# Forgetting attention moved whole out of RWKV's loop into the later projections, with its two products turned round

## The reference

```python
z = h @ w_in[i]
q = rmsnorm_2(q, g_qnorm[i]); k = rmsnorm_2(k, g_knorm[i])
for start in range(0, s_len, Q_BLOCK):            # Q_BLOCK = 128
    end = start + Q_BLOCK
    sc = einsum('bqhd,bkhd->bhqk', q[:, start:end], k[:, :end]) * scale
    sc = where(kpos <= qpos, sc + c[start:end] - c[:end], -1e30)   # c: running sum of log forget gates
    outs.append(einsum('bhqk,bkhd->bqhd', softmax(sc), v[:, :end]))
zr = zr + mu_shift[i] * (token_shift(zr) - zr)    # RWKV's columns, shifted by a token
... # RWKV: decay and a through two small products ("lora"), a recurrence over the tokens
merged = sigmoid(zg_fox) * (y_fox @ w_o_fox) + sigmoid(zg_rwkv) * (y_rwkv @ w_o_rwkv)
```

## Time and profile before

| | us |
|---|---|
| median of 3 runs | 4296.64 |
| the profiled execution | 4300.37 |
| its span | 4299.1 |
| TensorE busy | 3922.4 (91%) |
| VectorE busy | 2143.1 (50%) |
| ScalarE busy | 1157.1 (27%) |
| POOL busy | 330.0 (8%) |

### The profile page before, as it was taken

How to read it: one execution, slowest core, us unless ns; L and a number is a source line. 1 busy time by engine, 2 the same in 40 slices (tenths; PEclk the granted TensorE clock), 3 DMA queues, 4 the chain that set the end, 5 groups by cost and what they waited for, 6 DMA issues and landing times. The chain is left out here.

```text
span 4299.1 us, 75536 instructions
## 1 busy us (share of the span) xinstructions
PE 3922.4 (91%) x33542; PEld 3206.1 (75%) x33542; DVE 2143.1 (50%) x3525; ACT 1157.1 (27%) x1597; POOL 330.0 (8%) x362
## 2 busy tenths in 40 slices
PE   6999959986998999999999999778887999999999
PEld 5788837774876888888798677566666788888877
DVE  4633345554433444445624333465554476666774
ACT  4221234442322312121400222242323321111122
POOL 0001102230000000000000000232311000000000
PEclk8999969997998999999999899888787999999999
DMA  5212120114112111111132312201004311111111
GB/s 179 87 52 69 50 84 6 32 32 150 49 40 98 48 51 40 50 48 49 51 133 96 125 67 84 87 23 56 22 10 149 108 48 41 49 49 49 50 45 64
DMA packets 213721, 281.99 MB, mean 66 GB/s; under 512 B 15612, under 2 KB 171004, under 8 KB 213268
## 3 DMA queue, kind: packets, MB, share of 16 engines
q1 hardware_dynamic: 177536, 191.35, 13.8%
q10 hardware_dynamic: 35860, 85.79, 5.3%
HBM read 217.11 MB, written 60.00 MB: 64 GB/s over the span
## 5 line engine op out<-in xcount | busy, mean ns | idle before, releaser
L436 PE MATMUL ps<-sb_a_h,sb_whi 128*128 128x512 f32 x2912 | 1164.5, 400 | 51.0 <-DVE sb_a_h L665 44.6
L437 PE MATMUL ps<-sb_a_h,sb_wlo 128*128 128x512 f32 x2912 | 1146.1, 394 | 0.0
L438 PE MATMUL ps<-sb_a_h,sb_whi 128*128 128x512 f32 x2912 | 1145.5, 393 | 0.0
L436 PEld LDWEIGHTS ps<-sb_a_h,sb_whi 128*128 128x128 f32 x2912 | 552.8, 190 | 195.1 <-issue 53.3
L438 PEld LDWEIGHTS ps<-sb_a_h,sb_whi 128*128 128x128 f32 x2912 | 553.2, 190 | 118.6
L437 PEld LDWEIGHTS ps<-sb_a_h,sb_wlo 128*128 128x128 f32 x2912 | 553.5, 190 | 116.9 <-issue 4.3
L389 ACT ACTIVATE sb_whi<-sb_wraw 128x2048 fp32r<-128x2048 f32 (+3 forms) x146 | 260.4, 1783 | 839.7 <-PE ps L438 512.8
L397 DVE TENSOR_TENSOR sb_wlo<-sb_wraw,sb_whi 128x2048 fp32r<-128x2048 f32 (+3 forms) x146 | 315.8, 2163 | 241.5 <-ACT sb_whi L389 216.0
L548 DVE TENSOR_TENSOR sb_x<-sb_x,ps 128x512 f32<-128x512 f32 x480 | 313.3, 683 | 227.0 <-PE ps L438 224.5
L436 PE MATMUL ps<-sb_a_g,sb_whi 128*128 128x512 f32 x896 | 349.8, 390 | 10.5 <-DVE sb_x L548 10.5
L437 PE MATMUL ps<-sb_a_g,sb_wlo 128*128 128x512 f32 x896 | 348.8, 389 | 0.0
(11 more groups left out here) (513 smaller groups left out, 5567.2 us busy)
## 6 DMA issues: line engine op xcount, KB each, us to landing
sb_wraw<-w_in SPq DMA_DIRECT2D x33, 1024.0 KB, 5.1
sb_wraw<-w_ff SPq DMA_DIRECT2D x32, 1024.0 KB, 5.3
sb_wraw<-w_up SPq DMA_DIRECT2D x22, 1024.0 KB, 5.0
sb_wraw<-w_down SPq DMA_DIRECT2D x11, 1024.0 KB, 4.8
sb_wraw<-w_xkv SPq DMA_DIRECT2D x8, 1024.0 KB, 5.5
sb_wraw<-w_out SPq DMA_DIRECT2D x8, 1024.0 KB, 5.3
sb_a_f<-y ACTq DMA_DIRECT2D x16, 512.0 KB, 4.6
gates<-sb_a_f ACTq DMA_DIRECT2D x32, 256.0 KB, 2.0
```

Source lines behind the costliest of these rows:

```text
L436: e.matmul(o, wh[:, k, c], xh[:, sl], start=(k == 0), stop=False)
L437: e.matmul(o, wl[:, k, c], xh[:, sl], start=False, stop=False)
L438: m = e.matmul(o, wh[:, k, c], xl[:, sl], start=False, stop=(k == t.nk - 1))
```

## The change

It moves all of attention's steps into `a4`: beside the 25 shift tiles from the fourth on (`later = shift[3:]`) and the 32 gate tiles, four to a tile (after k = 1, 3, 5, 7), and leaves RWKV's `loop` without a side stream. In the value product it makes the values stationary (64 columns of the array for each head, the two heads of a pair one after the other for each 128 keys) and moves 128 columns of turned weights. For the turning it multiplies the weights by a diagonal matrix of the reciprocal row sums (`DG`, made by VectorE after the exponential) in place of a transpose; so the output comes out divided and already turned, and the division, the output's transposes and one step after each four blocks go. The generators have 55 steps a pair, 220 in all. The shift tiles and the lora products use 4 banks instead of 6 (attention has 4 to 7), the stores to DRAM 6 staging buffers instead of 8.

```diff
                 for t in shift:
-                    pe_fm(e, t, hp)
+                    pe_fm(e, t, hp, None, (0, 1, 2, 3), pe_fox, (1, 3, 5, 7) if t in later else ())
...
                 for t in gates:
-                    pe_fm(e, t, hp, None, (0, 1, 2, 3), pe_fox, (2, 5, 7))
+                    pe_fm(e, t, hp, None, (0, 1, 2, 3), pe_fox, (1, 3, 5, 7))
...
                     if t.first:
                         ve_cut(e, t.j + 2)
+                    if t in later:
+                        four(ve_fox)
...
+                for t in first[-2:]:
+                    e.wait_ge(*stored(t.key))
+                e.wait_ge(*x_spilled.at(0))
                 for t in shift:
...
-                sp_load(e, shift[-1].j + 3)
+                sp_load(e, shift[0].j + 3)
                 e.wait_ge(*x_spilled.at(0))
-                e.wait_ge(*bk.filled(shift[-1].key))
...
-                for t in gates:
+                for t in later + gates:
                     if t.first:
                         sp_load(e, t.j + 3)
-                    three(sp_fox)
+                    four(sp_fox)
...
                         if a == 0:
-                            e.wait_ge(*fx_exp[g].at(8 * p + qb))
+                            e.wait_ge(*fx_dg[g].at(8 * p + qb))
...
-                            m = e.transpose(ps[:, b:b + 128], lg_of(p, qb, g)[:, a + b:a + b + 128], C("ident"))
+                            m = e.matmul(ps[:, b:b + 128], lg_of(p, qb, g)[:, a + b:a + b + 128], DG[g], start=True, stop=True)
...
-                    for j in range(qb + 1):
-                        m = e.matmul(bk["fx_y", p, qb // 4][:, c:c + 64], lg_of(p, qb, g)[:, j * 128:(j + 1) * 128],
-                                     R(VF + j * 128 + g * 64, 64), start=(j == 0), stop=(j == qb))
+                for j in range(qb + 1):
+                    for g in range(2):
+                        m = e.matmul(bk[key][64 * g:64 * g + 64, c:c + 128], R(VF + j * 128 + g * 64, 64),
+                                     lg_of(p, qb, g)[:, j * 128:(j + 1) * 128], start=(j == 0), stop=(j == qb))
...
+                for g in range(2):
+                    e.wait_ge(*fx_exp[g].at(8 * p + qb))
+                    e.reciprocal(sinv[:, g:g + 1], R(SUM + (qb % 4) * 2 + g, 1)).then_inc(*vo.up())
+                    e.wait_ge(*vo.last())
...
+                    e.tensor_scalar(DG[g], C("ident"), sinv[:, g:g + 1], None, ALU.mult).then_inc(*fx_dg[g].up())
...
-            def loop(pre, inner, scan, fox):
-                fox = slow(fox)
+            def loop(pre, inner, scan):
...
-                    together(*streams, side=fox)
-                for _ in fox:
-                    pass
+                    together(*streams)
```

More of the change, by code:

```diff
@@ L441, in pe_fm @@
                 if k in at:
-                    next(side)
+                    next(side, None)
             if t.last:
@@ L2314, in stage, with four @@
             def stage(key):
-                return AF[:, 512 * (no[key] % 8):512 * (no[key] % 8 + 1)]
+                return AF[:, 512 * (no[key] % 6):512 * (no[key] % 6 + 1)]
             def room(key):
-                return s_o[no[key] % 8].at(no[key] // 8 - 1)
+                return s_o[no[key] % 6].at(no[key] // 6 - 1)
             def stored(key):
[L2321 to L2325, removed]
+                return s_o[no[key] % 6].at(no[key] // 6)
+            later = shift[3:]
+            def four(stream):
+                for _ in range(4):
+                    next(stream, None)
             def sums(e):
@@ L2420, in ve_a4 @@
                         ve_cut(e, t.j + 2)
-                    three(ve_fox)
+                    four(ve_fox)
                     e.wait_ge(*bk.filled(t.key))
@@ L2479, in ac_a4 @@
                     row = 512 * g + j * 128
-                    e.dma_start(S["rw_d"][row:row + 128, hf * 512:(hf + 1) * 512], stage(key)).then_inc(*s_o[no[key] % 8].up())
-                for t in first[-2:]:
-                    e.wait_ge(*stored(t.key))
+                    e.dma_start(S["rw_d"][row:row + 128, hf * 512:(hf + 1) * 512], stage(key)).then_inc(*s_o[no[key] % 6].up())
                 for t in gates:
@@ L2545, in b2, with av_done @@
             neg_gain, sinv = R(SUM + 8, 1), R(SUM + 16, 8)
-            r1, r2, cr = (R(F0 + (4 + j) * T, T, 0, 8) for j in range(3))
+            r1, r2, cr = (R(X0 + j * T, T, 0, 8) for j in (6, 7, 4))
             def lg_no(p, qb, g):
[L2551 to L2556, removed]
+                return 20 * p + 4 + 2 * qb + g
+            def av_done(p, qb):
+                return bk.filled(("fx_y", p, qb // 4)) if qb % 4 == 3 else fx_av.at((2 * p + qb // 4) * 3 + qb % 4)
             def lg_room(e, n):
@@ L2643, in ve_block @@
                 yield
+                for g in range(2):
+                    e.wait_ge(*fx_exp[g].at(8 * p + qb))
+                    e.reciprocal(sinv[:, g:g + 1], R(SUM + (qb % 4) * 2 + g, 1)).then_inc(*vo.up())
+                    e.wait_ge(*vo.last())
+                    if p or qb:
+                        last = (p, qb - 1) if qb else (p - 1, 7)
+                        e.wait_ge(*bk.filled(("fx_t", *last, g, chunks(last[1])[-1][0])))
+                    e.tensor_scalar(DG[g], C("ident"), sinv[:, g:g + 1], None, ALU.mult).then_inc(*fx_dg[g].up())
                 for a, n in chunks(qb):
@@ L2656, in ac_block @@
                     yield
-                if qb % 4 == 0 and (p or qb):
-                    e.wait_ge(*bk.emptied(("fx_y", p, 0) if qb else ("fx_y", p - 1, 1)))
                 for g in range(2):
+                    if p or qb >= 4:
+                        e.wait_ge(*fx_dg[g].at(8 * p + qb - 4))
                     lg, sm = lg_of(p, qb, g), sms[(2 * qb + g) % 4]
@@ L2711, in pe_fox @@
                             yield from pe_block(e, p, qb)
-                        yield
-                        yb = lgs[(22 * p + 12 + 9 * qh) % 4]
-                        ps = bk.take(("fx_yt", p, qh), FB)
-                        e.wait_ge(*bk.emptied(("fx_y", p, qh)))
-                        e.wait_ge(*bk.room(("fx_yt", p, qh)))
-                        for j in range(4):
-                            m = e.transpose(ps[:, j * 128:(j + 1) * 128], yb[:, j * 128:(j + 1) * 128], C("ident"))
-                        m.then_inc(*bk.fill(("fx_yt", p, qh)))
                         yield
@@ L2847, in b2 @@
             a4(*fox)
+            for stream in fox:
+                for _ in stream:
+                    pass
             meet()
```

87 lines of the change are left out of this document (36 added, 51 removed).

## The result

Four runs of the changed kernel took 4428.31 to 4435.4 us, median 4431.38; four of the kernel before 4293.16 to 4302.06, median 4298.8. The ratio is 1.031 (95% interval 1.0293 to 1.0328): 132 us slower, where 41 were forecast. The way was right, the size was not, and the time lies above the range. The profiled execution took 4433.03 us (span 4431.7).

A forecast was written before the change was run, and what follows sets the result against it. Projections were taken as dense on TensorE, RWKV's loop as half work, half waiting. +105 work, +71 waits, +15 clock, -150 from the loop made +41 us: 4336 us stated, range 4235 to 4400 (the forecast's own 4305 to 4375).

The forecast's parts named there:

- Part 1, TensorE's work: Projections: attention's TensorE work there, breaks included, goes from 60 to 165 us, +105 us (+88 to +140).
- the base: Gates' stretch before the change, read from 2450 us: 60 us of TensorE's own time for attention, 14 idle.
- rival 3: Value product: no overlap, the two heads run one after the other, +32 us more, 4368; chance within the forecast's 0.45.
- Part 2, waits: Projections: TensorE's waits with attention's steps four to a tile, 85 us against 14, +71 us (+20 to +100).
- its clock: Projections: three of the cuts' waits bring half clock for 10 us each, +15 us (0 to +50).
- The cuts: Projections: 14 cuts of weights on VectorE and ScalarE delay attention's steps, most by 2 to 5 us, 35 us (15 to 45).
- Part 3, what the loop gives back: RWKV's loop without attention: units of 45 us (40 to 52) instead of 63, -150 us (-185 to -100).
- rival 2: Waits and clock: waits at most cuts, projections' clock about 0.85, loop's 0.7, +120 us, 4416; chance 0.12.
- The floor: RWKV's loop: turns of one shared bank pair, 15 + 21 = 36 us a unit that can't go below.
- Rival 1: Loop gives more than projections take: waits 35 us, no clock lost, units of 42, -46 us, 4250; chance 0.36.
- What would show it: Signs: diagonal and value records 0.11 apart, fourth shift tile to barrier +190 us, some 85 us waits, units 45 us apart.

The follow-up runs named there:

- e2: Kernel before with only the new products (values stationary, weights turned by the diagonal), attention placed as before; 4330.11 us, ratio 1.0061 to the kernel before.
- e6: Changed kernel with VectorE's and ScalarE's cuts of weights put behind the tile's four attention steps; 4394.78 us, ratio 1.0207 to the kernel before.
- e5: Changed kernel with two bank pairs for one and four single banks for two for RWKV's products; 4367.65 us, ratio 1.0163 to the kernel before.
- e12: Changed kernel with scores ahead, cuts late, two bank pairs and two more blank steps in each norm chain; 4301.23 us, ratio 0.9998 to the kernel before.
- e11: Changed kernel with scores ahead, cuts late, two bank pairs and attention's steps in twos after k = 3 and 7; 4356.89 us, ratio 1.0116.

## Why the prediction was right in its way and wrong in its size

In the prediction's own terms, with the dense matmuls' lengthening told apart by the clock (a dense matmul of the trace at full clock, over the 0.2265 us of the earlier trace rows, is a break; at half clock, the clock), the change in us:

| | forecast | measured |
|---|---|---|
| TensorE's work in the projections, at full clock | +105 | +117 |
| waits there | +71 | +56 |
| clock there | +15 | +30 |
| before the loop's first product, and "lora" | 0 | +10 |
| what the loop gives back | -150 | -81 |

**Part 1, TensorE's work: the products right, the base low.** 0.11 us a record of the turning and 0.11 for two records of the values (0.115 measured) came as forecast, so rival 3 (no overlap) falls. The two heads' halves run side by side at 128 moving columns too, and a multiplication by a diagonal costs two records where a transpose costs one. The 165 us of the forecast stand beside 165 for attention's instructions in the balance, but that is luck. The forecast is at full clock and includes what breaks cost the dense matmuls; the 165 of the balance include 14 us of half clock and leave out 33 us of breaks. Like for like it was 184. The base explains it: the stretch for the gates was read from 2450 us, and their first matmul starts earlier:

```profile
2438.41 0.79 PE L436 MATMUL ps<-sb_a_h,sb_whi 128*128 128x512 f32 x1
```

So TensorE's own part before was not 60 us but, at full clock, 67, and the prediction's own scaling gives (67 - 34)/0.42 = 79 for its 62, and 182 for 165. e2 shows the form's net loss in the old place: its TensorE time was less (184 for 196 us in both stages), and the wait for VectorE took it back.

**Part 2, waits: right in sum; its clock: too small.** 85 us of waits were forecast, and there were 75 before attention's instructions and 4 more elsewhere (79). The cuts were put at 35, and the eight long waits that end behind a cut make 38. Taking the cuts out of the way (e6) removed 19 us of waits and as much again of clock and other time. The clock was put at 15 us, from "three of them at half clock for 10 us"; there were ten long waits and 83 us more at half clock (119 - 36). The dense matmuls took 38 us more: 20 at full clock, from 144 breaks for 62, and 18 at half clock; attention's own lost 11 more by it. The Trainium skill (TensorE: Matmul & The Clock Gate, "HAM oscillation") says that repeated idle gaps throttle each next stretch; the trace agrees, with 0.51 for 7 us around a wait of 5.07 us, and the prediction used it for its rival only. The 8 us more before the loop's first product were not foreseen at all.

**Part 3, what the loop gives back: the step that failed.** "I take 45 a unit (40 to 52)". It was 51.8, in the steady units 54.6, and the loop gave back 81 us, not 150: 69 of the 91 us by which the sum was short. Attention's share was read rightly (140 + 30 forecast, 139 + 30 by the trace). What failed is the conversion: taking out 169 us of work and waits from a shared engine returned 81. The loop was called "half work and half waiting", but its own row has TensorE busy 354 of 442 us. 49 of the missing 87 are the clock (twice as many of RWKV's records at the lower level); 38 are waits that attention had filled. The banks could shorten both (e5: waits 92 for 122, instructions 305 for 329); the inverse's chain stays. The text did say that "TensorE's clock may fall with less work", and gave it no price: from the earlier trace rows, 354 us busy at 0.81 with attention's part in it, it should have had one. At 0.7, as rival 2 has it, RWKV's 281 us become 281 x 0.81/0.71 = 321 by the two measured clocks; the trace says 329. The floor was also summed a little low (six turns of 2.7 us are 16, not 15), and 4341 less 3.8 is 4337, not 4336; neither changes anything.

**The rivals.** Rival 2, "waits and clock" (4416, chance 0.12), has the mechanism that happened: 0.91 and 0.95 in the projections for its 0.85, 0.71 in the loop for its 0.7, long waits behind eight of the fourteen cuts. That its time comes within 15 us is partly luck: it had 95 us more of waits (56 measured) and 45 of clock (30), and even it took -125 for the loop. Rival 1 needed a unit under 43 us, and no run came under 44.1 (e12, by the mean of the instruction above), with two bank pairs.

**What would show it** was right to name the unit's length: at 51.8 us for 45 the seven units alone miss 48 us. The stretch from the fourth shift tile to the barrier was to grow by 190 and grew by some 212.

**Open.** A second pair of banks in the kernel before was not tried, as attention holds those banks there. Why the form costs 45 us in the new place and 26 in the old is not separated further, nor is the pair of banks from the single ones. And two attention waits of 1.7 and 1.9 us in the projections, like the one of 2.3 us before, left the clock as it was, while six of 1.8 to 2.6 us came with half clock; what tells them apart no run shows.

## What to carry to other kernels

When work is moved out of a stage that waits, price what it leaves behind from both sides: its own time goes, but the rest can run at a lower clock (here 0.71 for 0.81) and meets its waits bare; of 169 us taken out, 81 came back. When it is moved into a dense stage, walk each step of the other engines' in-order queues: a block's small steps belong ahead of the long ones (the cuts' 1.9 + 2.3 us), and a step that a product waits for should not be added to the engine that is late. And ask what the separation allows: the banks that came free were worth 62 us, the largest single gain, and were not part of the change (whether the kernel before could have gained from more banks, with attention in the loop, is not known).

## What the runs showed of the hardware that was not expected

- Matmuls that nobody reads raised the loop's granted clock from 0.71 to 0.95, and RWKV's own held TensorE 241 us for 329; but the filler's 120 us left a net gain of 14 (about the measurement's limit), and with shorter gaps a loss of 20.
- A change between dense 128x512 matmuls and attention's small products cost 0.2 to 0.26 us each at full clock (62 breaks, 12.6 us in the kernel before; 62 fewer, 16 us in e11).
- Each wait of 3.6 to 5.8 us in a dense stage came with 3 to 7 us at half clock, and so did six of 1.8 to 2.6 us: in all 55 us more of waits before attention's instructions came with 83 us more at half clock.
- Two products of 64 output rows, each on one half of the array, took 0.115 us for two records at 128 moving float32 columns: the time of one (0.11).
